# Two instruction orders at the four joins between blocks: products taken whole once both operand halves are there, and VectorE's update chain two tiles deep

## The chip, the cores and the metric

The kernel runs on one core of a Trainium2 chip. The metric is the device time of one execution, in microseconds; below it is given as the median of three runs. Five engines work side by side, each through its own list of instructions: TensorE (PE, the matmuls; PEld is its loading of weights), VectorE (DVE), ScalarE (ACT), GpSimd (POOL) and SyncE (SP, which here only starts transfers). They meet by semaphores: an instruction can wait until a counter has reached a value, and raise one when it is done.

## The reference

The computation is three transformer layers on 512 tokens of width 1024, in float32: layer A (gated delta net and memory attention), layer B (stick-breaking attention and memory attention), and layer C (pooling, differential attention, cross attention). In layers A and B each of the two halves ends in a residual step of this form:

```
y = jnp.concatenate([mix, cross], axis=-1) @ w_out[i]
x = x + rms_norm(y, norm_post_mix[i])
h = rms_norm(x, norm_pre_mlp[i])
y = jnp.square(jax.nn.relu(h @ w_up[i])) @ w_down[i]
x = x + rms_norm(y, norm_post_mlp[i])
```

So `y` is normalised over the tokens' 1024 values, added to `x`, and the new `x`, normalised again, is the operand of the next large product. There are four such joins: after A's output projection (`A.post`, before `A.mlp`), after A's MLP (`A.post2`, before `B.qk`), after B's output projection (`B.post`, before `B.mlp`) and after B's MLP (`B.post2`, before `C.u`). The change concerns these four alone.

## The kernel before

Activations are held turned: 1024 features are 8 tiles (index k, `KD` = 8) of 128 partitions by 512 tokens. `XT` is x, `Y` the output of the last product. Weights come in units of 1024x256 numbers; unit u uses buffers `STG`, `WH`, `WL` number u mod 2, and gives two output tiles (j = 0, 1), each in its own PSUM bank of 128x512.

To keep float32 accuracy with the faster matmul type, each operand is split in a high and a low part: `WH` and `WL` for weights, `HH` and `HL` for activations. A product of one tile k is three matmuls: `HH` with `WH`, `HL` with `WH`, and `HH` with `WL`. A unit is 2 x 8 x 3 = 48 matmuls of 512 columns.

A join runs like this. TensorE sums squares of y over features (`sum_tokens`: eight short matmuls on `SQA`, eight on `SQ`), ScalarE takes the root, VectorE the reciprocal `RSC`, and TensorE spreads it over all partitions into PSUM bank 4 (`spread_tokens`). Then for each k: VectorE scales y (`scaled`, a scalar_tensor_tensor that reads `Y` and bank 4 and writes PSUM bank 5 or 6; line 2008 in the profile, `PS<-Y,PAR,PS`), adds it to x (line 2011, `XT<-XT,PS`); ScalarE makes `HH` of the new tile (line 1330, `HH<-XT,PAR`) and its square for the next norm; VectorE makes `HL` (`operand_lo`, line 2008, `HL<-XT,PAR,HH`). GpSimd meanwhile makes the low weights of unit u+1 (line 421, `WL<-STG,WH`) and then adds up the squares (lines 411 and 415, `SQA`).

Since the sum over features of x is not known until all of x is, the next product is made of x without its norm, and the norm's factor is multiplied in as the result leaves PSUM. TensorE takes units u and u+1 together there (`product_pair`, for the units named in `PAIRED`): as tile k of the operand arrives it does tile k of both outputs of unit u, and one tile-step of unit u+1, so 9 matmuls for each k. After k = 7 come the other eight tile-steps of unit u+1 (n = 8 to 15), and between them the sum (`sum_tokens`) and the spreading (`spread_tokens`) of the next norm. ScalarE copies the spread factor to `RS`, and VectorE then empties the banks of unit u (in an MLP, line 2008, `RR<-PS,RS`). Unit u+2 (`product`) writes to the banks of unit u, and waits until its first one is empty.

The order on each engine is written out by hand in the program; there is no scheduler. In `product_pair` each k is in two parts: `of_hi` waits for `HH` of tile k and does the six matmuls that need it alone, `of_lo` waits for `HL` and does the other three.

Of the kernel before, what the change touches and what calls it, by code (L numbers as in the profile page):

```python
# [27 lines left out]
ALU = mybir.AluOpType  # L28
# [3 lines left out]
P = 128  # L32
S = 512
D = 1024
KD = D // P
# [78 lines left out]
def program(nc, ws, xt_in, memt_in, memt2_in, par_in, con_in, rope_in, rcnt_in, out):  # L114
    ctx = ExitStack()
    with ctx:
        def sb(name, shape, dt=F32, scope=ctx, align=32):
            return scope.enter_context(nc.sbuf_tensor(name, shape, dt, align_bytes=align))

        sems = {}  # L120
# [22 lines left out]
        HL = sb("HL", [P, KD, S], F32R, align=2048)  # L143
        HH = sb("HH", [P, KD, S], F32R)
        XT = sb("XT", [P, KD, S])
        STG = [sb(f"STG{i}", [P, KD, UC]) for i in range(2)]
        WH = [sb(f"WH{i}", [P, KD, UC], F32R) for i in range(2)]
        WL = [sb(f"WL{i}", [P, KD, UC], F32R) for i in range(2)]
        Y = sb("Y", [P, KD, S])
# [10 lines left out]
        PS = ctx.enter_context(nc.psum_tensor("PS", [P, 8, 512], F32))  # L160
# [5 lines left out]
        def par(name, i=0, n=1):  # L166
            return PAR[:, PCOL[name] + i:PCOL[name] + i + n]
# [149 lines left out]
        def emptied(kind, u, j, i=None, step=0):  # L317

            return lin(EMPTIED[kind][u] + j + 1, 2 * step, i)
# [14 lines left out]
        def bcast_done(n):  # L334
            return NORMS.index(n) + 1
# [4 lines left out]
        def split_done(q, k):  # L340
            return 8 * SPLITS.index(q) + k + 1
# [139 lines left out]
        def _(pe):  # L481
            I_ = con("ident")

            def mm(o, l, r, start, stop, **kw):
                return pe.matmul(o, l, r, start=start, stop=stop, **kw)  # L485

            def sum_tokens(name, nt=NB):

                m = SQ_BASE[name] + KD - 1
                pe.wait_ge(sems["sqa"], 6 * sums_done(name))  # L490
                before = [x for x in NORMS if SUMS.index(x) < SUMS.index(name)]
                copied = sum(1 for x in before if x not in POSTS)
                if copied:
                    pe.wait_ge(sems["rs"], copied)
                if before and before[-1] in POSTS:
                    pe.wait_ge(sems["y_scaled"], 8 * POSTS.index(before[-1]) + KD)
                for b in range(nt):
                    mm(PS[:, 4, b:b + 1], blk(SQA[:, :], b), con("ones")[:, 0:1], b == 0, False, skip_group_check=True)
                pe.wait_ge(sems["sq"], m + 1)
                for b in range(nt):  # L500
                    last = mm(PS[:, 4, b:b + 1], blk(SQ[:, m % 4, :], b), con("ones")[:, 0:1], False, True,
                              skip_group_check=True)
                last.then_inc(sems["ss"], 1)

            def spread_tokens(name, nt=NB):

                pe.wait_ge(sems["rsc"], sums_done(name))
                for b in range(nt):
                    last = mm(PS[:, 4, b * P:(b + 1) * P], RSC[:, b:b + 1].to_broadcast([P, P]), I_, True, True)
                last.then_inc(sems["bc"], 1)  # L510

            def wait_bank(u, j, i=None, step=0):

                if u >= 2:
                    kind = KIND[u - 2]
                    pe.wait_ge(sems[f"emptied_{kind}"], emptied(kind, u - 2, j, i, step))
# [42 lines left out]
            def projection(name, split=None, norm=None, after=None, halfway=None, order=range(KD), behind=None, x=(HH, HL)):  # L559


                def fn(u, i, step):
                    r = u - U0[name]
                    first = r == 0 and i is None
                    if first and name in PAIRED:
                        return product_pair(u, split)
                    if r == 1 and name in PAIRED:
                        return
                    product(u, i, step, x[0], x[1],
                            split=(lambda k: split_done(split, k)) if first and split else None,  # L570
                            between=(lambda: spread_tokens(norm)) if norm and r == 1 and i is None else None,
                            tiles=1 if name == "A.bg" else 2, halfway=halfway if first else None, order=order,
                            behind=behind if first else None)
                    if norm and first:
                        sum_tokens(norm)
                    if after and r:
                        after(r - 1)
                run_phase(pe, name, fn)
                if after:
                    after(NU[name] - 1)  # L580

            def product_pair(u, q):

                pe.wait_ge(sems["lo"], u + 1)
                for v in (u, u + 1):
                    wait_bank(v, 0)
                    wait_bank(v, 1)

                def of_hi(v, j, k):
                    bank = PS[:, 2 * (v % 2) + j, :]  # L590
                    wh, wl = WH[v % 2][:, k, j * P:(j + 1) * P], WL[v % 2][:, k, j * P:(j + 1) * P]
                    mm(bank, wh, HH[:, k, :], k == 0, False)
                    mm(bank, wl, HH[:, k, :], False, False)

                def of_lo(v, j, k):
                    bank = PS[:, 2 * (v % 2) + j, :]
                    last = mm(bank, WH[v % 2][:, k, j * P:(j + 1) * P], HL[:, k, :], False, k == KD - 1)
                    if k == KD - 1:
                        last.then_inc(sems["tile"], 1)

                for k in range(KD):
                    pe.wait_ge(sems["hh"], split_done(q, k))
                    of_hi(u, 0, k)
                    of_hi(u, 1, k)
                    if k == 0:
                        pe.wait_ge(sems["lo"], u + 2)
                    of_hi(u + 1, k % 2, k // 2)
                    pe.wait_ge(sems["hl"], split_done(q, k))
                    of_lo(u, 0, k)
                    of_lo(u, 1, k)  # L610
                    of_lo(u + 1, k % 2, k // 2)
                for n in range(KD, 2 * KD):
                    of_hi(u + 1, n % 2, n // 2)
                    of_lo(u + 1, n % 2, n // 2)
                    if n == KD:
                        sum_tokens(q)
                    if n == KD + 4:
                        spread_tokens(q)

            def memory_rows(u, xh, xl, split=None):  # L620
# [1385 lines left out]
        def _(dve):  # L2006
            def stt(o, a, s_, b, op0, op1):
                return dve.scalar_tensor_tensor(out=o, in0=a, scalar=s_, in1=b, op0=op0, op1=op1)  # L2008

            def tt(o, a, b, op):  # L2010
                return dve.tensor_tensor(o, a, b, op)  # L2011
# [7 lines left out]
            def operand_lo(q, src, gain, hh=HH, hl=HL, n=S, k0=0, k1=KD):  # L2019
                for k in range(k0, k1):  # L2020
                    dve.wait_ge(sems["hh"], split_done(q, k))
                    stt(hl[:, k, 0:n], src[:, k, 0:n], par(gain, k), hh[:, k, 0:n].bitcast(F32), ALU.mult, ALU.subtract)\
                        .then_inc(sems["hl"], 1)

            def invert(name, nt=NB):
                dve.wait_ge(sems["sqrt"], sums_done(name))
                dve.reciprocal(RSC[:, 0:nt], RT[:, 0:nt]).then_inc(sems["rsc"], 1)
# [87 lines left out]
            def post_and_operand(post, gain, q, gain_in):  # L2115

                invert(post)
                dve.wait_ge(sems["bc"], bcast_done(post))
                if post in ("A.post", "B.post"):
                    dve.wait_ge(sems["emptied_act"], emptied("act", U0[post[0] + ".out"] + 3, 1))  # L2120
                n = 8 * POSTS.index(post)
                def scaled(k):
                    if k >= 2:
                        dve.wait_ge(sems["x_new"], n + k - 1)
                    stt(PS[:, 5 + k % 2, :], Y[:, k, :], par(gain, k), PS[:, 4, :], ALU.mult, ALU.mult)\
                        .then_inc(sems["y_scaled"], 1)

                scaled(0)
                for k in range(KD):
                    dve.wait_ge(sems["y_scaled"], n + k + 1)  # L2130
                    tt(XT[:, k, :], XT[:, k, :], PS[:, 5 + k % 2, :], ALU.add).then_inc(sems["x_new"], 1)
                    if k + 1 < KD:
                        scaled(k + 1)
                    operand_lo(q, XT, gain_in, k0=k, k1=k + 1)

            def half_top(a, i):
                e, n = i % 2, 8 * a + i
# [354 lines left out]
            for r in range(NU["A.gate"]):  # L2492
                u = U0["A.gate"] + r
# [200 lines left out]
            for r in range(NU["C.out"]):  # L2694
                u = U0["C.out"] + r
# [134 lines left out]
```

## Time and profile before

| | us |
|---|---|
| median of three runs | 2205.88 |
| lowest and highest | 2205.38, 2208.51 |
| profiled execution, its own time | 2205.38 |
| profiled execution, span of the trace | 2203.6 |

| engine | busy, share of the span |
|---|---|
| TensorE, matmuls | 96% |
| TensorE, weight loads | 80% |
| VectorE | 49% |
| ScalarE | 34% |
| GpSimd | 8% |

The profile records one execution. The span is 1.8 us shorter than that execution's own time. TensorE is busy for nearly the whole of it, so what matters is where it is not, and where it is busy at a lower clock: the profile gives the granted clock for any stretch, as a share of full speed (0.50 is the 1.2 GHz level, 1.00 the 2.4 GHz one). The four joins lie at about 417 to 450, 777 to 811, 1054 to 1087 and 1415 to 1447 us of the span.

### The profile page before, as it was taken

The numbers are of one execution on the slowest core, as the hardware profiler recorded it, in microseconds if no ns is written. First come the engines' busy times: TensorE is split into PE (matmuls) and PEld (weight loads), VectorE is DVE, ScalarE is ACT, GpSimd is POOL, SyncE is SP. The second block draws the span as 40 slices with busy tenths as digits, with TensorE's granted clock in tenths as the row PEclk, the third lists the DMA queues.
The fourth block names the chain that finished last, engine by engine and source line by source line (L and its number), as shares of the span: only waits on it lengthen the run. The fifth ranks groups of instructions, "written<-read, shape, count | busy, mean of one in ns | idle before, by whom it ended". The sixth has DMA issues, their size and how long they took to land.

```text
span 2203.6 us, 28778 instructions
## 1 busy us (share of the span) xinstructions
PE 2125.9 (96%) x11819; PEld 1753.5 (80%) x11819; DVE 1084.5 (49%) x1381; ACT 751.0 (34%) x1033; POOL 177.1 (8%) x141
## 2 busy tenths in 40 slices
PE   7999999999999999999999999999899999999998
PEld 6886888788888878767788888787688868888886
DVE  4664555454454453353645445455765335454453
ACT  5444432432122232574422222323462243222222
POOL 2000220300000120001300000401001000000001
PEclk9999999999999999999999999999999999999999
DMA  6231000222222222101222222232132202322221
GB/s 239 77 114 39 22 21 1 77 96 96 95 95 95 97 75 96 39 1 58 76 97 96 95 98 94 104 125 86 58 134 77 81 35 78 113 96 95 95 95 58
DMA packets 27025, 182.81 MB, mean 83 GB/s; under 512 B 2992, under 2 KB 3120, under 8 KB 5424
## 3 DMA queue, kind: packets, MB, share of 16 engines
q1 hardware_dynamic: 25200, 174.07, 22.2%
q10 hardware_dynamic: 1296, 4.71, 0.5%
q0 software_dynamic: 432, 2.62, 0.3%
q8 instruction: 74, 1.21, 0.2%
q14 instruction: 23, 0.19, 0.0%
HBM read 179.30 MB, written 2.10 MB: 82 GB/s over the span
## 4 chain that ended last, share of the span: by engine, by line
PE 89%; DVE 6%; ACT 3%; issue 1%; DMA 0%; POOL 0%; ACTq 0%; DVEq 0%; POOLq 0%; SPq 0%
PE PS L485 88%; ACT Y L1330 1%; DVE Y L2008 1%; ACT WH L1330 1%; DVE WL L2011 1%; DVE Y L2011 1%; DVE SQ L2011 0%; DMA STG<-weights 0%; PE PS L696 0%; DVE DMX L2620 0%; DVE HL L2011 0%; POOL SQA L415 0%; ACT ABUF L1330 0%; ACT SQ L1330 0%; DVE QKV L2011 0%
## 5 line engine op out<-in xcount | busy, mean ns | idle before, releaser
L485 PE MATMUL PS<-HH,WH 128*128 128x512 f32 (+1 forms) x1608 | 635.2, 395 | 17.4 <-ACT HH L1330 10.1
L485 PE MATMUL PS<-HH,WL 128*128 128x512 f32 (+1 forms) x1608 | 625.0, 389 | 0.0
L485 PE MATMUL PS<-HL,WH 128*128 128x512 f32 (+1 forms) x1608 | 613.1, 388 | 0.0
L2011 DVE TENSOR_TENSOR WL<-STG,WH 128x2048 fp32r<-128x2048 f32 (+1 forms) x163 | 367.1, 2252 | 287.0 <-ACT WH L1330 287.0
L1330 ACT ACTIVATE WH<-STG 128x2048 fp32r<-128x2048 f32 (+2 forms) x171 | 314.8, 1841 | 525.9 <-PE PS L485 523.8
L485 PEld LDWEIGHTS PS<-HH,WH 128*128 128x128 f32 x1608 | 305.8, 190 | 90.3 <-issue 22.7
L485 PEld LDWEIGHTS PS<-HH,WL 128*128 128x128 f32 x1608 | 305.9, 190 | 61.3
L485 PEld LDWEIGHTS PS<-HL,WH 128*128 128x128 f32 x1608 | 304.9, 190 | 62.2 <-issue 2.2
L485 PE MATMUL PS<-UPH,WH 128*128 128x512 f32 x832 | 324.2, 390 | 1.4 <-DVE UPL L2008 1.4
L485 PE MATMUL PS<-UPH,WL 128*128 128x512 f32 x832 | 323.7, 389 | 0.0
L485 PE MATMUL PS<-UPL,WH 128*128 128x512 f32 x832 | 323.7, 389 | 0.0
L485 PEld LDWEIGHTS PS<-UPH,WH 128*128 128x128 f32 x832 | 156.2, 188 | 34.1 <-DVE UPL L2008 1.8
L485 PEld LDWEIGHTS PS<-UPH,WL 128*128 128x128 f32 x832 | 156.2, 188 | 32.5
L485 PEld LDWEIGHTS PS<-UPL,WH 128*128 128x128 f32 x832 | 156.2, 188 | 32.3
L411 POOL TENSOR_TENSOR SQA<-SQ 128x512 f32<-128x512 f32 (+1 forms) x14 | 24.9, 1778 | 1594.2 <-ACT SQ L1330 1594.2
L2008 DVE SCALAR_TENSOR_TENSOR RR<-PS,RS 128x512 f32<-128x512 f32 x96 | 66.3, 690 | 146.3 <-PE PS L485 138.4
L2011 DVE TENSOR_TENSOR Y<-Y,PS 128x512 f32<-128x512 f32 x64 | 43.9, 687 | 180.2 <-PE PS L485 180.2
L1330 ACT ACTIVATE UPH<-RR 128x512 fp32r<-128x512 f32 x64 | 40.5, 632 | 226.7 <-DVE RR L2008 226.7
L2011 DVE TENSOR_TENSOR XT<-XT,PS 128x512 f32<-128x512 f32 x80 | 54.6, 683 | 120.2 <-PE PS L485 120.1
L415 POOL TENSOR_TENSOR SQA<-SQA,SQ 128x512 f32<-128x512 f32 (+1 forms) x70 | 97.5, 1393 | 145.2 <-ACT SQ L1330 141.7
L1330 ACT ACTIVATE Y<-PS 128x512 f32<-128x512 f32 (+5 forms) x96 | 61.6, 646 | 86.8 <-PE PS L485 72.1
L2011 DVE TENSOR_TENSOR RQ<-RR 128x512 f32<-128x512 f32 x96 | 66.4, 692 | 3.3
(286 smaller groups left out, 2015.0 us busy)
## 6 DMA issues: line engine op xcount, KB each, us to landing
STG<-weights SPq DMA_DIRECT2D x163, 1024.0 KB, 4.8
XT<-x_t ACTq DMA_DIRECT2D x2, 1024.0 KB, 12.6
out_t<-Y SPq DMA_DIRECT2D x8, 256.0 KB, 2.0
STG<-weights SPq DMA_DIRECT2D x4, 256.0 KB, 5.5
MX<-mem_t ACTq DMA_DIRECT2D x4, 256.0 KB, 7.5
CON<-consts ACTq DMA_DIRECT2D x1, 1024.0 KB, 18.2
Y<-recip_counts POOLq DMA_DIRECT2D x1, 1024.0 KB, 5.0
KVM<-mem_t POOLq DMA_DIRECT2D x1, 1024.0 KB, 8.4
```

The source lines that it names most:

```text
L411: pool.tensor_tensor(SQA[:, 0:n], SQ[:, base % 4, 0:n], SQ[:, (base + 1) % 4, 0:n], ALU.add).then_inc(sems["sqa"], 1)
L415: pool.tensor_tensor(SQA[:, 0:n], SQA[:, 0:n], SQ[:, (base + k) % 4, 0:n], ALU.add).then_inc(sems["sqa"], 1)
L485: return pe.matmul(o, l, r, start=start, stop=stop, **kw)
L1330: return act.activation(o, i, f, **kw)
L2008: return dve.scalar_tensor_tensor(out=o, in0=a, scalar=s_, in1=b, op0=op0, op1=op1)
L2011: return dve.tensor_tensor(o, a, b, op)
```

## The change

Two functions are written in another order. No instruction of arithmetic is added or taken away.

In `product_pair` the two parts become one, `step`: three matmuls for one tile-step in the order `HH` with `WH`, `HL` with `WH`, `HH` with `WL`. Each k waits once, for `HL` of tile k. The sum of the next norm stands after n = 9 (was after 8), its spreading after n = 14 (was after 12).

In `post_and_operand` VectorE's loop runs `scaled` one tile ahead of the addition, and the addition two tiles ahead of `operand_lo`. Before, the addition of tile 0 stood right behind `scaled(0)`, and `operand_lo(k)` right behind `scaled(k + 1)`.

```diff
-                def of_hi(v, j, k):
+                def step(v, j, k):
                     mm(bank, wh, HH[:, k, :], k == 0, False)
-                    mm(bank, wl, HH[:, k, :], False, False)
-
-                def of_lo(v, j, k):
-                    bank = PS[:, 2 * (v % 2) + j, :]
-                    last = mm(bank, WH[v % 2][:, k, j * P:(j + 1) * P], HL[:, k, :], False, k == KD - 1)
+                    mm(bank, wh, HL[:, k, :], False, False)
+                    last = mm(bank, wl, HH[:, k, :], False, k == KD - 1)
...
                 for k in range(KD):
-                    pe.wait_ge(sems["hh"], split_done(q, k))
-                    of_hi(u, 0, k)
-                    of_hi(u, 1, k)
+                    pe.wait_ge(sems["hl"], split_done(q, k))
+                    step(u, 0, k)
+                    step(u, 1, k)
                     if k == 0:
                         pe.wait_ge(sems["lo"], u + 2)
-                    of_hi(u + 1, k % 2, k // 2)
-                    pe.wait_ge(sems["hl"], split_done(q, k))
-                    of_lo(u, 0, k)
-                    of_lo(u, 1, k)
-                    of_lo(u + 1, k % 2, k // 2)
+                    step(u + 1, k % 2, k // 2)
                 for n in range(KD, 2 * KD):
-                    of_hi(u + 1, n % 2, n // 2)
-                    of_lo(u + 1, n % 2, n // 2)
-                    if n == KD:
+                    step(u + 1, n % 2, n // 2)
+                    if n == KD + 1:
                         sum_tokens(q)
-                    if n == KD + 4:
+                    if n == 2 * KD - 2:
                         spread_tokens(q)
...
-                scaled(0)
-                for k in range(KD):
-                    dve.wait_ge(sems["y_scaled"], n + k + 1)
-                    tt(XT[:, k, :], XT[:, k, :], PS[:, 5 + k % 2, :], ALU.add).then_inc(sems["x_new"], 1)
-                    if k + 1 < KD:
-                        scaled(k + 1)
-                    operand_lo(q, XT, gain_in, k0=k, k1=k + 1)
+                for k in range(KD + 2):
+                    if k < KD:
+                        if k >= 2:
+                            dve.wait_ge(sems["x_new"], n + k - 1)
+                        stt(PS[:, 5 + k % 2, :], Y[:, k, :], par(gain, k), PS[:, 4, :], ALU.mult, ALU.mult)\
+                            .then_inc(sems["y_scaled"], 1)
+                    if 1 <= k <= KD:
+                        dve.wait_ge(sems["y_scaled"], n + k)
+                        tt(XT[:, k - 1, :], XT[:, k - 1, :], PS[:, 5 + (k - 1) % 2, :], ALU.add).then_inc(sems["x_new"], 1)
+                    if k >= 2:
+                        operand_lo(q, XT, gain_in, k0=k - 2, k1=k - 1)
```

VectorE at the start of a join (`A.post`), before. `PS<-Y` is `scaled`, `XT<-XT,PS` the addition, `HL` is `operand_lo`; the names in brackets are the semaphores waited for:

```order
L2008 SCALAR_TENSOR_TENSOR PS<-Y,PAR,PS 128x512 [waits emptied_act,bc]
L2011 TENSOR_TENSOR XT<-XT,PS 128x512 [waits y_scaled]
L2008 SCALAR_TENSOR_TENSOR PS<-Y,PAR,PS 128x512
L2008 SCALAR_TENSOR_TENSOR HL<-XT,PAR,HH 128x512 [waits hh]
L2011 TENSOR_TENSOR XT<-XT,PS 128x512 [waits y_scaled]
```

The same place with the change:

```order
L2000 SCALAR_TENSOR_TENSOR PS<-Y,PAR,PS 128x512 [waits emptied_act,bc]
L2000 SCALAR_TENSOR_TENSOR PS<-Y,PAR,PS 128x512
L2003 TENSOR_TENSOR XT<-XT,PS 128x512 [waits y_scaled]
L2000 SCALAR_TENSOR_TENSOR PS<-Y,PAR,PS 128x512 [waits x_new]
L2003 TENSOR_TENSOR XT<-XT,PS 128x512 [waits y_scaled]
L2000 SCALAR_TENSOR_TENSOR HL<-XT,PAR,HH 128x512 [waits hh]
```

`HL` of tile 0 stood behind one addition and two `scaled`; now it stands behind two additions and three `scaled`, and the third of these waits for the first addition.

TensorE at the start of the pair that follows, before (`WH0`, `WL0` are the buffers of unit u, `WH1`, `WL1` those of unit u+1):

```order
L485 MATMUL PS<-CON,RSC 128x128 x3
L485 MATMUL PS<-HH,WH0 128x512 [waits emptied_act,hh,lo]
L485 MATMUL PS<-HH,WL0 128x512
L485 MATMUL PS<-HH,WH0 128x512
L485 MATMUL PS<-HH,WL0 128x512
L485 MATMUL PS<-HH,WH1 128x512 [waits lo]
L485 MATMUL PS<-HH,WL1 128x512
L485 MATMUL PS<-HL,WH0 128x512 [waits hl]
```

And with the change:

```order
L485 MATMUL PS<-CON,RSC 128x128 x3
L485 MATMUL PS<-HH,WH0 128x512 [waits emptied_act,hl,lo]
L485 MATMUL PS<-HL,WH0 128x512
L485 MATMUL PS<-HH,WL0 128x512
L485 MATMUL PS<-HH,WH0 128x512
L485 MATMUL PS<-HL,WH0 128x512
L485 MATMUL PS<-HH,WL0 128x512
L485 MATMUL PS<-HH,WH1 128x512 [waits lo]
```

Six matmuls stood ahead of the wait for `hl`; now all nine stand behind it.

TensorE from the spreading of the next norm to the first matmul of unit u+2, before (`CON,RSC` is the spreading, `WH0` now unit u+2):

```order
L485 MATMUL PS<-CON,RSC 128x128 [waits rsc]
L485 MATMUL PS<-CON,RSC 128x128 x3
L485 MATMUL PS<-HH,WH1 128x512
L485 MATMUL PS<-HH,WL1 128x512
L485 MATMUL PS<-HL,WH1 128x512
L485 MATMUL PS<-HH,WH1 128x512
L485 MATMUL PS<-HH,WL1 128x512
L485 MATMUL PS<-HL,WH1 128x512
L485 MATMUL PS<-HH,WH1 128x512
L485 MATMUL PS<-HH,WL1 128x512
L485 MATMUL PS<-HL,WH1 128x512
L485 MATMUL PS<-HH,WH0 128x512 [waits emptied_dve,lo]
```

With the change:

```order
L485 MATMUL PS<-CON,RSC 128x128 [waits rsc]
L485 MATMUL PS<-CON,RSC 128x128 x3
L485 MATMUL PS<-HH,WH1 128x512
L485 MATMUL PS<-HL,WH1 128x512
L485 MATMUL PS<-HH,WL1 128x512
L485 MATMUL PS<-HH,WH0 128x512 [waits emptied_dve,lo]
```

Between the spreading and the wait for the emptied bank stood nine matmuls; now there are three.

## Rows read from the trace of the kernel before

**Rows 1.** The chain that ended last, by engine, from the page.

```profile
PE 89%; DVE 6%; ACT 3%; issue 1%; DMA 0%; POOL 0%; ACTq 0%; DVEq 0%; POOLq 0%; SPq 0%
```

**Rows 2.** TensorE's waits: what for, us in total, times, longest.

```profile
PE PS L485 <- ACT HH L1330: 10.1, 4, 2.6
```

**Rows 3.** Timeline of TensorE, starts of the four pairs: start, us, instruction, [idle before].

```profile
422.81 0.76 PE L485 MATMUL PS<-HH,WH 128*128 128x512 f32 x1 [2.55 <-ACT HH L1330]
...
783.79 0.77 PE L485 MATMUL PS<-HH,WH 128*128 128x512 f32 x1 [2.47 <-ACT HH L1330]
...
1059.72 0.77 PE L485 MATMUL PS<-HH,WH 128*128 128x512 f32 x1 [2.56 <-ACT HH L1330]
...
1420.95 0.77 PE L485 MATMUL PS<-HH,WH 128*128 128x512 f32 x1 [2.48 <-ACT HH L1330]
```

**Rows 4.** Timeline of VectorE, start of the first join.

```profile
420.37 0.76 DVE L2008 SCALAR_TENSOR_TENSOR PS<-Y,PAR,PS 128x512 f32<-128x512 f32 x1 [1.32 <-ACT Y L1330]
421.16 0.69 DVE L2011 TENSOR_TENSOR XT<-XT,PS 128x512 f32<-128x512 f32 x1
421.77 0.75 DVE L2008 SCALAR_TENSOR_TENSOR PS<-Y,PAR,PS 128x512 f32<-128x512 f32 x1
422.70 2.25 DVE L2008 SCALAR_TENSOR_TENSOR HL<-XT,PAR,HH 128x512 fp32r<-128x512 f32 x1 [0.18 <-ACT HH L1330]
424.87 0.67 DVE L2011 TENSOR_TENSOR XT<-XT,PS 128x512 f32<-128x512 f32 x1
...
426.33 0.75 DVE L2008 SCALAR_TENSOR_TENSOR HL<-XT,PAR,HH 128x512 fp32r<-128x512 f32 x1
427.00 0.68 DVE L2011 TENSOR_TENSOR XT<-XT,PS 128x512 f32<-128x512 f32 x1
```

**Rows 5.** Timeline of GpSimd, low weights of unit u+1 at the four joins.

```profile
419.86 4.54 POOL L421 TENSOR_TENSOR WL<-STG,WH 128x2048 fp32r<-128x2048 f32 x1 [6.50 <-ACT WH L1330]
...
779.99 4.52 POOL L421 TENSOR_TENSOR WL<-STG,WH 128x2048 fp32r<-128x2048 f32 x1 [6.34 <-ACT WH L1330]
...
1056.76 4.52 POOL L421 TENSOR_TENSOR WL<-STG,WH 128x2048 fp32r<-128x2048 f32 x1 [6.50 <-ACT WH L1330]
...
1417.49 4.52 POOL L421 TENSOR_TENSOR WL<-STG,WH 128x2048 fp32r<-128x2048 f32 x1 [6.34 <-ACT WH L1330]
```

**Rows 6.** Timeline of TensorE, two neighbours early in the first pair.

```profile
423.37 0.63 PE L485 MATMUL PS<-HH,WL 128*128 128x512 f32 x1
423.80 0.63 PE L485 MATMUL PS<-HH,WH 128*128 128x512 f32 x1
```

**Rows 7.** One stretch early in the first pair: us, TensorE busy, granted clock, DMA.

```profile
423.00:424.00 1.00, 1.00 (x3) 0.50 0.00 0
```

**Rows 8.** Timeline of TensorE, first matmuls of the next norm's sum, four pairs.

```profile
442.08 0.95 PE L485 MATMUL PS<-CON,SQA 128*128 128x1 f32 x8
...
803.40 0.95 PE L485 MATMUL PS<-CON,SQA 128*128 128x1 f32 x8
...
1079.58 0.95 PE L485 MATMUL PS<-CON,SQA 128*128 128x1 f32 x8
...
1439.66 0.95 PE L485 MATMUL PS<-CON,SQA 128*128 128x1 f32 x8
```

**Rows 9.** Timeline of TensorE, the spreading and the first matmuls of unit u+2.

```profile
446.65 1.05 PE L485 MATMUL PS<-CON,RSC 128*128 128x128 f32 x8
...
449.62 0.39 PE L485 MATMUL PS<-HH,WH 128*128 128x512 f32 x1
449.84 0.39 PE L485 MATMUL PS<-HL,WH 128*128 128x512 f32 x1
```

**Rows 10.** Timeline of ScalarE and VectorE behind that spreading.

```profile
447.74 0.60 ACT L1330 ACTIVATE RS<-PS 128x512 f32<-128x512 f32 x1 [3.51 <-PE PS L485]
...
448.37 0.69 DVE L2008 SCALAR_TENSOR_TENSOR RR<-PS,RS 128x512 f32<-128x512 f32 x1 [2.54 <-ACT RS L1330]
```

**Rows 11.** Timeline of GpSimd, its first addition of squares.

```profile
426.89 1.34 POOL L411 TENSOR_TENSOR SQA<-SQ 128x512 f32<-128x512 f32 x1 [2.50 <-ACT SQ L1330]
```

More of the change, by code:

```diff
@@ L2121, in post_and_operand @@
                 n = 8 * POSTS.index(post)
-                def scaled(k):
-                    if k >= 2:
-                        dve.wait_ge(sems["x_new"], n + k - 1)
-                    stt(PS[:, 5 + k % 2, :], Y[:, k, :], par(gain, k), PS[:, 4, :], ALU.mult, ALU.mult)\
-                        .then_inc(sems["y_scaled"], 1)
-                scaled(0)
-                for k in range(KD):
-                    dve.wait_ge(sems["y_scaled"], n + k + 1)
-                    tt(XT[:, k, :], XT[:, k, :], PS[:, 5 + k % 2, :], ALU.add).then_inc(sems["x_new"], 1)
-                    if k + 1 < KD:
-                        scaled(k + 1)
-                    operand_lo(q, XT, gain_in, k0=k, k1=k + 1)
+                for k in range(KD + 2):
[7 more added lines that the diff above has]
+                        tt(XT[:, k - 1, :], XT[:, k - 1, :], PS[:, 5 + (k - 1) % 2, :], ALU.add).then_inc(sems["x_new"], 1)
+                    if k >= 2:
+                        operand_lo(q, XT, gain_in, k0=k - 2, k1=k - 1)
             def half_top(a, i):
```

## The prediction

> **What bounds the kernel now.** I read the shares of the chain that ended last first. TensorE has 89% of it [rows 1], so the change can act only where TensorE idles, waits or runs slowly. Next came TensorE's waits. The largest group is exactly the place that the change rewrites: four waits for `HH`, 10.1 us together, one at the start of each pair [rows 2, 3]. Then I read the timelines of that place. After its start the pair shows no further idle time: from the first matmul to the first one of the next norm's sum TensorE has 75 matmuls of 512 columns (9 for each of eight k, 3 for n = 8), and takes 19.27, 19.61, 19.86 and 18.71 us for them in the four places [rows 3, 8]. At the full rate of 0.227 us each (0.22 to 0.23 between neighbours [rows 9]) 75 would take 17.03. The rest, 2.24, 2.58, 2.83 and 1.68 us, in all 9.33, is the low clock at the start: the granted clock is 0.50 there, the 1.2 GHz level, after a wait of 2.5 us and short matmuls before it [rows 3, 7], and neighbours stand 0.43 us apart [rows 6].
>
> VectorE delivers one tile of `HL` each 2.13 us (from one addition to the next, 424.87 to 427.00 [rows 4]); TensorE at full rate uses one in 9 x 0.227 = 2.04. So the supply is a little slower than the use. But TensorE has lost 1.7 to 2.8 us at the low clock, against 7 x 0.09 = 0.6 us that the supply falls behind over seven tiles. TensorE's own work sets the pair's end, and that end moves with its start.
>
> **Term 1, the later start.** The first matmul waited for `HH` of tile 0; now it waits for `HL` of tile 0, which VectorE also reaches later. Call T0 the start of `scaled(0)`, 420.37 in the first place [rows 4]. The first matmul came at T0 + 2.44 [rows 3, 4]. I take the same 2.44 in the other places, so T0 is 781.35, 1057.28 and 1418.51 there. Spacing on VectorE: from an `HL` to the addition behind it 0.67, from an addition to the next instruction 0.61 [rows 4]; `scaled` is of the same form as `HL`, so I take 0.67 behind it. In the new order:
> - `scaled(0)` at T0, `scaled(1)` at T0 + 0.67, the first addition at T0 + 1.34, ended at T0 + 2.03 (0.69 long).
> - `scaled(2)` waits for that end (about 0.03 more, as between the first two rows): T0 + 2.06. The second addition at T0 + 2.73.
> - `HL` of tile 0 at T0 + 3.33. It needs `HH`, which is there 1.54 after the start of the first addition (421.16 to 422.70 [rows 4]), so at T0 + 2.88: no wait.
> - Unhindered it takes 0.75, to T0 + 4.08. TensorE starts about 0.11 after what it waits for (422.70 to 422.81 [rows 3, 4]): T0 + 4.19, or 1.75 later than before.
>
> In the row this instruction took 2.25 and not 0.75: it ended at 424.95, that is 0.55 after the end of GpSimd's `WL` at 424.40 [rows 4, 5]. The new start, 423.70 in the first place and 1060.61 in the third, still lies inside GpSimd's instruction (to 424.40 and 1061.28), so the end stays at 424.95 and becomes 1061.83. TensorE then starts at 425.06 and 1061.94, which is 2.25 and 2.22 later. In the second place GpSimd ends at 784.51, before 784.68: 1.75. In the fourth it ends at 1422.01, just behind 1421.84, and 0.55 after that is 1422.56, as good as the unhindered end of 1422.59: 1.75. Sum 2.25 + 1.75 + 2.22 + 1.75 = 8.0 us. Bounds: 7.0 if nothing holds `HL` (4 x 1.75), 9.0 if all four are held as long as the first (4 x 2.25).
>
> The Trainium skill (SBUF — State Buffer, "SBUF: two separate sides") says that a VectorE instruction with two SBUF inputs and a GpSimd instruction that reads SBUF lock each other out for the whole instruction, whichever began first. The 2.25 us row agrees. By that rule the new order has a second collision, weighed as a rival below.
>
> **The clock after the start.** The wait ahead of the pair grows from 2.5 to some 4.5 us, so the clock is low at the start as before. What the low clock costs I take as before, 9.33 in all, so nothing in the sum. Bounds from the same rows: the least place four times is 4 x 1.68 = 6.7 (2.6 less), the dearest 4 x 2.83 = 11.3 (2.0 more).
>
> **What the shorter VectorE cycle brings.** `HL(k)` no longer stands waiting for `HH(k)`: 0.61 + 0.67 + 0.67 = 1.95 a tile in place of 2.13. Over seven tiles that is 1.3 us, but it comes on an engine that TensorE does not wait for once it has started. I count nothing. Having one wait per k in place of two is also nothing: neither kind shows idle time behind the first.
>
> **Term 2, the spreading moved to the end.** Unit u+2 writes the bank that VectorE empties, and VectorE needs `RS`, which ScalarE copies after the spreading. From the start of the spreading S (446.65) the copy starts at S + 1.09, the emptying at S + 1.72 and ends at S + 2.41 [rows 9, 10]. With 0.1 for TensorE's reaction, the bank is free at S + 2.51. Before, TensorE wanted it at 449.62, S + 2.97 [rows 9]: hidden, by 0.46. Two tile-steps (6 x 0.23 = 1.38) now stand ahead of the spreading and not behind it, so it wants it at S + 1.59. A stall of 0.92 appears, four times: 3.7 us. Queued behind the waiting matmul is all of TensorE's further work. Bounds: 4 x 0.8 = 3.2 with no reaction time, and 4 x 1.2 = 4.8 if some more comes late. The sum one tile-step later costs nothing: the reciprocal hangs on VectorE's `WL` of unit u+2, and the spreading moved by more than the sum did.
>
> **Sum.** 8.0 + 3.7 = 11.7 us. The profiled execution took 2205.38, with a span of 2203.6 and 1.8 around it that stays. That gives 2217.1. The median of the runs shown is 0.5 higher; I say 2217.3.
>
> **The rivals.**
> - *The clock rises at the same moment as before, however late TensorE starts.* Then of a later start only the part that would have run at full rate is lost: a matmul done at the low rate would have taken 0.43 and is done later in 0.227, so 0.227 / 0.43 = 0.53 of the delay remains, 8.0 x 0.53 = 4.2. With term 2: 7.9, 2213.3. For it: the low stretch differs between places (1.68 to 2.83) though the wait ahead of them is the same. Against: it would have to hold in all four. Chance 12%.
> - *The stall in front of unit u+2 does not come*, because the bank is released sooner than the rows say: only term 1, 2213.4. Against: the copy and the emptying are one chain behind the spreading, with 2.41 us in a row each. Chance 6%.
> - *VectorE meets GpSimd's additions of squares.* An addition of squares starts 2.02 after x of its tile does and takes 1.34 (424.87 to 426.89 [rows 4, 11]), so until + 3.36. Before, `HL(k)` began at + 1.46, ahead of it. Now it comes 1.95 + 0.61 = 2.56 after, inside it. Held as in the first row, it ends at + 3.91 and not at + 3.31; two cycles then take 4.5, so 2.25 a tile. `HL(7)` comes 15.8 after `HL(0)`, and TensorE's step k = 7 stands 12 matmuls ahead of the sum, so 16.0 to 17.1 after its start: still in time. It decides from about 2.3 a tile on. Were every cycle held by a further 0.6, so 2.8, `HL(7)` would come at 19.6, on average 3 us late: 4 x 3 more, 2229. Chance 4%. This is the lock of the Trainium skill's page again; by its rule each `HL` but the first and last is held once, which is the harmless case.
> - *The other side, not slower: the end of each pair is set by the last `HL`.* Then the shorter cycle ends it 7 x (2.13 - 1.95) = 1.3 us sooner where `HL(0)` ends when it did (first and third place), and at best so in all four: - 5.2, with term 2 added - 1.5, 2203.9. For it: 2.13 is more than 2.04. Against: it decides only where the low clock costs less than 0.6 us, and the least is 1.68; and even wholly at full rate, 17.03 after its new start, the pair in the first place would be at 442.09, where it was at 442.08. Chance 3%.
>
> **How the numbers follow.** The forecast has 75%, the rivals 12, 6, 4 and 3. Range: the lower bounds give 7.0 - 2.6 + 3.2 = 7.6, 2213.0; the upper ones 9.0 + 2.0 + 4.8 = 15.8, 2221.2. That takes in the first two rivals. What a measurement can tell from no change is about 0.2%, 4.4 us: slower by more than that means over 2210.3. All cases but the last lie above it; a clock that comes back sooner together with a smaller stall could end inside it. Slower 92%, within 5%, faster 3%.
>
> **What would show it.** TensorE's wait at the start of each pair now ends on VectorE's `HL`, near 4.8 us in the first and third place and 4.2 in the others. `HL(0)` starts 1.0 later against T0, with 2.25 shrunk to about 1.25 in the first place. Four new waits of 0.9 stand in front of unit u+2, on VectorE's first emptying. VectorE's cycle is 1.95, or 2.25 if GpSimd's additions hold it. The distance from a pair's first matmul to its sum is the old one plus one tile-step of 0.68. The prediction is wrong if that distance shrinks by more than a microsecond a place, if TensorE waits inside the eight steps, or if the bank is free when it asks.

## The result, and the profile after

The changed kernel took 2229.09 us (median of 4 runs, 2225.30 to 2230.28) against 2206.73 (4 runs): ratio 1.0096, 95% interval 1.0081 to 1.0111. Slower, as forecast, but by 22 us where 11.7 were forecast, and outside the range. The sign and both terms of the sum were right; the step that failed, the one that took everything outside the joins as fixed, is told below. The profiled execution is quicker than every timed run: 2221.33, with a span of 2219.5 against 2203.6, so 15.9 more.

TensorE's waits after, the rows that answer to [rows 2] (what for, us, times, longest):

```profile
PE PS L485 <- DVE HL L2000: 19.1, 5, 4.8
...
PE PS L485 <- DVE RR L2000: 1.6, 2, 0.8
...
PE PS L485 <- DVE QKB L2000: 0.8, 1, 0.8
PE PS L485 <- DVE UT L2003: 0.8, 1, 0.8
```

The four waits for `HH` are gone. In their place are four longer waits for `HL`, 18.2 us together (the fifth of that row, 0.9, stood in the kernel before too), and four new ones of 0.8 for VectorE's first emptying of a bank. The timeline of TensorE shows the four starts, to set against [rows 3]:

```profile
427.18 0.77 PE L485 MATMUL PS<-HH,WH 128*128 128x512 f32 x1 [4.81 <-DVE HL L2000]
...
791.60 0.77 PE L485 MATMUL PS<-HH,WH 128*128 128x512 f32 x1 [4.23 <-DVE HL L2000]
...
1069.83 0.76 PE L485 MATMUL PS<-HH,WH 128*128 128x512 f32 x1 [4.40 <-DVE HL L2000]
...
1433.44 0.77 PE L485 MATMUL PS<-HH,WH 128*128 128x512 f32 x1 [4.81 <-DVE HL L2000]
```

VectorE in the first join, against [rows 4]:

```profile
422.48 1.41 DVE L2000 SCALAR_TENSOR_TENSOR PS<-Y,PAR,PS 128x512 f32<-128x512 f32 x2 [1.32 <-ACT Y L1322]
423.80 0.68 DVE L2003 TENSOR_TENSOR XT<-XT,PS 128x512 f32<-128x512 f32 x1
424.51 0.76 DVE L2000 SCALAR_TENSOR_TENSOR PS<-Y,PAR,PS 128x512 f32<-128x512 f32 x1
425.18 0.68 DVE L2003 TENSOR_TENSOR XT<-XT,PS 128x512 f32<-128x512 f32 x1
425.78 1.26 DVE L2000 SCALAR_TENSOR_TENSOR HL<-XT,PAR,HH 128x512 fp32r<-128x512 f32 x1
```

T0 is 422.48. `HL` starts at T0 + 3.30 (forecast 3.33) and TensorE at T0 + 4.70 (4.69). The 1.26 us of `HL` are GpSimd's hold again, now shorter, because `HL` comes later. The first matmuls of the next norm's sum, against [rows 8]:

```profile
447.70 0.95 PE L485 MATMUL PS<-CON,SQA 128*128 128x1 f32 x8
...
810.90 0.95 PE L485 MATMUL PS<-CON,SQA 128*128 128x1 f32 x8
...
1089.91 0.95 PE L485 MATMUL PS<-CON,SQA 128*128 128x1 f32 x8
...
1452.67 0.94 PE L485 MATMUL PS<-CON,SQA 128*128 128x1 f32 x8
```

These come 20.52, 19.30, 20.08 and 19.23 us after their pair's start. The sum now stands one tile-step (0.68) later, so like for like 19.84, 18.62, 19.40 and 18.55, against 19.27, 19.61, 19.86 and 18.71: 1.0 us less in all. And the end of the first pair, against [rows 9]:

```profile
452.94 1.05 PE L485 MATMUL PS<-CON,RSC 128*128 128x128 f32 x8
...
455.50 0.47 PE L485 MATMUL PS<-HH,WH 128*128 128x512 f32 x1 [0.80 <-DVE RR L2000]
```

From the spreading to unit u+2 it takes 2.56, where 2.51 was forecast, and 0.80 of it is idle.

Cut at the same landmarks (first matmul of the norm's sum ahead of a join; first matmul of unit u+2 behind it, which before is the spreading + 2.97), the traces of the kernel before (this one and e8_before_copy) and of the changed kernel (this one, e5_full_again, e9_full_third) read:

| stretch | before, two traces | changed, three traces | difference of means |
|---|---|---|---|
| start to first join | 416.64, 420.29 | 418.74, 415.55, 424.46 | varies |
| join 1 | 32.98, 32.97 | 36.76, 36.65, 36.65 | + 3.7 |
| join 2 | 34.91, 34.89 | 36.63, 36.61, 36.63 | + 1.7 |
| join 3 | 33.58, 33.54 | 36.31, 36.23, 36.19 | + 2.7 |
| join 4 | 33.67, 33.67 | 36.22, 36.19, 36.22 | + 2.5 |
| between the joins | 895.4, 895.4 | 895.8, 895.9, 895.8 | + 0.4 |
| behind join 4 | 756.4, 756.3 | 759.0, 759.0, 759.0 | + 2.7 |

All but the first line repeats to 0.1 us or so. It adds up to 13.7 us for the change: 10.7 in the joins, 0.4 between them, 2.7 behind them. The first line is 13.5 us wide over all the traces of this study, and no line of the change acts there.

### The profile page after: what moved, and what is told of

It reads as the page before. It is cut to its first block, busy times and chain, and to the rows that moved or that the text cites. A ratio compares the mean times of both kernels' runs of the same rounds, so it can differ in the third digit from the quotient of the medians.

```text
span 2219.5 us, 28778 instructions
## 1 busy us (share of the span) xinstructions
PE 2127.8 (96%) x11819; PEld 1755.6 (79%) x11819; DVE 1087.5 (49%) x1381; ACT 750.5 (34%) x1033; POOL 176.7 (8%) x141
## 3 DMA queue, kind: packets, MB, share of 16 engines
q1 hardware_dynamic: 25200, 174.07, 22.4%
## 4 chain that ended last, share of the span: by engine, by line
PE 88%; DVE 6%; ACT 3%; issue 1%; DMA 1%; POOL 0%; ACTq 0%; DVEq 0%; POOLq 0%; SPq 0%
PE PS L485 87%; ACT Y L1322 2%; DVE Y L2000 1%; ACT WH L1322 1%; DVE Y L2003 1%; DVE WL L2003 1%; DMA MX<-mem_t 0%; DVE SQ L2003 0%; DVE PS L2000 0%; DMA STG<-weights 0%; PE PS L688 0%; DVE HL L2000 0%; DVE DMX L2610 0%; DVE HL L2003 0%; POOL SQA L415 0%
## 5 line engine op out<-in xcount | busy, mean ns | idle before, releaser
L485 PE MATMUL PS<-HL,WH 128*128 128x512 f32 (+1 forms) x1608 | 624.7, 388 | 0.0
L2003 DVE TENSOR_TENSOR XT<-XT,PS 128x512 f32<-128x512 f32 x80 | 54.5, 681 | 121.7 <-PE PS L485 121.7
```

## The experiments

For the first four experiments three theories stood against each other. L: the joins cost what the prediction says, and the low clock behind the longer wait costs the rest. V: VectorE's new order is what costs. N: the excess over the joins is chance of the runs. From e5_full_again on two took their place. P: the joins cost 10.8, and the rest of the first measurement is low clock in the stage ahead of the first join, where nothing was changed. E: an excess of 9 us over the joins belongs to the change.

**e1_pe_only.** TensorE's part of the change, VectorE in the old order:

```diff
...
                 for k in range(KD):
-                    pe.wait_ge(sems["hh"], split_done(q, k))
+                    pe.wait_ge(sems["hl"], split_done(q, k))
...
-                    if n == KD + 4:
+                    if n == 2 * KD - 2:
```

> TensorE's part alone (whole steps behind one wait for HL, later sum and spreading), VectorE in the old order. Theory L (later start, late spreading, and a dearer low clock behind the longer wait): the first matmul comes 2.2, 1.4, 2.2, 1.7 us later than before (7.5 in all), unit u+2 waits 0.8 four times (3.2), and the timed runs lie above that sum by most of what the full change lies above it: 2218 to 2228. Theory V (VectorE's new order is what costs): under 2212. Theory N (the excess over the joins is chance of the runs and not of the change): 2217.5.

Measured 2220.63 against 2210.01, ratio 1.0074 (1.0051 to 1.0097). The starts were 2.25, 1.40, 2.24 and 2.32 later against T0, 8.2 in all; the joins took 146.5 us, 11.4 more than before. The 11.4 are these 8.2 and the late spreading, 3.8, less 0.6 by which T0 comes sooner in the fourth join, so TensorE's part alone makes the whole cost in the joins, and theory V is out. What VectorE's old order could give back (it reaches `HL` of tile 0 sooner) was lost in the first, third and fourth join to GpSimd's hold: in the first, `HL` of tile 0 is asked for at T0 + 2.32 and takes 2.22 us.

```profile
423.33 2.22 DVE L2000 SCALAR_TENSOR_TENSOR HL<-XT,PAR,HH 128x512 fp32r<-128x512 f32 x1 [0.18 <-ACT HH L1322]
```

**e2_dve_only.** VectorE's part, TensorE in the old order:

```diff
...
-                scaled(0)
-                for k in range(KD):
...
+                for k in range(KD + 2):
...
```

> VectorE's part alone, TensorE in the old order. Theory L: HH of tile 0 is ready 0.55 us later, so four starts move by 0.55: 2.2 us, 2209, and no dearer clock since the wait is only 3 us. Theory V: 2216 or more. If the shorter VectorE cycle brings something here, it is under 2206.

Measured 2216.64 against 2210.01, ratio 1.0025 (1.0006 to 1.0045); joins 138.6, 3.5 more. The starts were 0.52 later in each place (2.1 in all, 2.2 expected). The expected 2209 was missed, and 2216 was theory V's number. But the kernel before ran 3.3 us slower here than the expectations assume: as a difference the time, some 5.5 us with an interval from 1.3 to 9.9, lies between theory L's 2.3 and theory V's 9.3 and takes in both. The trace speaks for the small cost. TensorE waited 3.00 to 3.08 us for `HH` in place of 2.5:

```profile
432.61 0.77 PE L485 MATMUL PS<-HH,WH 128*128 128x512 f32 x1 [3.07 <-ACT HH L1330]
```

**e3_old_places.** The changed kernel, sum and spreading where they stood before:

```diff
-                    if n == KD + 1:
+                    if n == KD:
...
-                    if n == 2 * KD - 2:
+                    if n == KD + 4:
```

> The changed kernel, but with the sum and the spreading of the next norm where they stood before (after n = 8 and n = 12). Theory L: the four waits of 0.80 us in front of unit u+2 go, 3.2 us less than the full change: some 2224 to 2226 against 2227 to 2229. If the late spreading were behind the excess too, it is under 2220.

Measured 2222.21, ratio 1.0055 (1.0034 to 1.0076). No wait in front of unit u+2 was left; joins 143.3, 2.4 less than the changed kernel (3.2 expected). The times alone don't settle it: 12.2 us over the kernel before, with an interval from 7.5 to 16.8, takes in the 13.3 below which the late spreading would be behind the excess, and lies under theory L's 17.3 to 19.3. The trace does: putting sum and spreading back saves 2.4 us in the joins, not the 10.7 by which the first measurement stood over the forecast.

**e4_places_only.** The kernel before with only the places moved:

```diff
-                    if n == KD:
+                    if n == KD + 1:
...
-                    if n == KD + 4:
+                    if n == 2 * KD - 2:
```

> The kernel before, with only the places of sum and spreading moved (after n = 9 and n = 14). Theory L: four waits of 0.8 us and nothing else, 2210. If the late spreading is behind the excess: 2214 or more.

Measured 2215.18, ratio 1.0015 (0.9998 to 1.0032), which can't be told from no change; joins 137.8, 2.7 more. The moved places cost 3.8 by themselves, but T0 came 0.9 us sooner in the second join and 0.6 sooner in the fourth. The wait is there in each place, alone and of the forecast size:

```profile
457.73 1.05 PE L485 MATMUL PS<-CON,RSC 128*128 128x128 f32 x8
460.29 0.47 PE L485 MATMUL PS<-HH,WH 128*128 128x512 f32 x1 [0.81 <-DVE RR L2008]
```

In this batch the kernel before ran 22 times, from 2203.93 to 2216.75: 13 us wide, where its first four runs lay within 3.1. The expectations of this batch are reckoned from 2206.7, its median in the first measurement; the differences are what can be compared.

**e5_full_again.** The changed kernel once more, without an edit.

> The changed kernel itself, once more, beside more runs of the kernel before. Theory P (the joins cost 10.8 us as the first trace shows, the rest of the first measurement is the low clock in the stage before the first join, which no line of the change touches and which falls differently from run to run): the ratio comes out near 1.005 to 1.007, the times of both kernels scatter by 10 us or more, and in this trace too the four joins from the first sum to unit u+2 take 10 to 12 us more than before, while the arrival at the first join follows the low-clock time ahead of it at about 0.46 us per us. Theory E (the excess of 9 us over the joins belongs to the change): the ratio is 1.009 or more again.

Measured 2223.42 against 2210.29, ratio 1.0066 (1.0040 to 1.0092); joins 145.7. Theory P's value; theory E's 1.009 lies inside the interval too, so this alone settles nothing. The arrival at the first join was 415.55, 3.2 us earlier than in the first trace of the same kernel.

**e6_keep_before** and **e7_keep_full.** Extra matmuls in TensorE's waits of the joins, in the kernel before and in the changed one (`keep(22)` there behind the spreading):

```diff
             def finish_post(name):
                 sum_tokens(name)
...
+                def keep(n):
+                    for _ in range(n):
+                        mm(PS[:, 7, 0:UC], WH[u % 2][:, 0, 0:P], WH[u % 2][:, 1, :], True, True)
+
+                keep(3)
                 spread_tokens(name)
+                keep(12)
```

> The kernel before, with extra matmuls (128 weights, 256 columns, results unused, bank 7) in TensorE's waits at each join: 3 ahead of the wait for the reciprocal, 12 behind the spreading. They take some 0.11 us each at the full rate and 0.21 at the low one. If they hold the clock up, the 75 matmuls of the pair take 17.0 us in place of 18.7 to 19.9, the starts move by at most 0.5 each, and the kernel gains 5 to 9 us. If the clock falls all the same, it loses 0 to 2 us.

> The changed kernel with the same extra matmuls, 22 behind the spreading since the wait is longer. If they hold the clock up, the later start (8.0) and the wait in front of unit u+2 (3.2) stand alone: 11 us more than e6_keep_before and about 1 to 4 more than the kernel before. If the low clock behind the longer wait were what makes the change dear (theory L's excess), the gain here is larger than in e6_keep_before by several us.

e6_keep_before: 2214.45, ratio 1.0009 (0.9993 to 1.0025). The expectation (5 to 9 us gained) failed in an instructive way. The clock did stay high in the first three joins, and in the first (first row: us, busy time of PE, PEld, DVE, ACT, POOL, granted clock, DMA share, GB/s) the pair was not shorter:

```profile
429.00:449.00 20.00, 18.82 (x80) 13.93 (x80) 15.74 (x21) 10.45 (x17) 13.44 (x8) 1.00 0.16 53
```

```profile
429.28 0.47 PE L485 MATMUL PS<-HH,WH 128*128 128x512 f32 x1 [1.11 <-ACT HH L1343]
...
430.96 0.51 PE L485 MATMUL PS<-HH,WH 128*128 128x512 f32 x1 [0.51 <-POOL WL L421]
...
432.87 0.51 PE L485 MATMUL PS<-HH,WH 128*128 128x512 f32 x1 [0.39 <-ACT HH L1343]
...
448.57 0.95 PE L485 MATMUL PS<-CON,SQA 128*128 128x1 f32 x8
```

448.57 - 429.28 is 19.29, at the full rate all along; before it was 19.27 with a start at the low one. TensorE now waits for GpSimd's low weights and for `HH` of the next tile instead: VectorE's cycle of 2.14 us a tile paces the pair. In the second and third pair, also at the full rate, the distance to the sum is 18.42 and 18.74, 1.2 and 1.1 less than before, with the same 2.14 a tile; there GpSimd holds `HL` of tile 0 for less. In the fourth the clock fell all the same (granted 0.50 from 1428 to 1430 us), and its distance is 19.62, 0.9 more. All four joins together took 133.7, 1.4 less than before.

e7_keep_full: 2219.61, ratio 1.0036 (1.0017 to 1.0055); joins 141.7, 4 less than the changed kernel and 8.0 more than e6_keep_before (11 expected); against the kernel before it takes some 8 us more, where 1 to 4 were expected. Its pairs reach the sum 18.52, 18.55, 19.42 and 18.50 after their start, 0.68 of it the moved sum. In the first, second and fourth the clock stayed high: about 17.85 like for like, 0.8 over the 17.03 of matmuls alone. In the third it fell (granted 0.50 from 1076 to 1078 us). So the extra matmuls gave 4.0 us here and 1.4 in the kernel before: the low clock behind the longer wait is dearer by 2.6 us over four joins, not by 9. Theory L falls.

**e8_before_copy** and **e9_full_third.** Both kernels without an edit, side by side.

> The kernel before against itself. It shows how far two sets of runs of one kernel lie apart, and gives a second trace of its joins. Theory P: the ratio is 1.000 with an error of about 0.002, the four joins take 134 to 137 us from first sum to unit u+2 (135.1 in the first trace), and the rest of the span follows the low-clock time outside the joins. Theory E needs a ratio within 0.001 of 1, so that 9 us of excess in the first measurement can't be chance.

> The changed kernel a third time, beside the copy of the kernel before. Theory P: joins 145 to 147 us, ratio 1.0045 to 1.007, and against runs of the kernel before at the same mean clock 11 us more. Theory E: 1.009 or more.

e8_before_copy: ratio 1.0004 (0.9989 to 1.0019), joins 135.1 as in the first trace. That ratio is what both theories asked for. e9_full_third: 2224.10 against 2209.93, ratio 1.0059 (1.0039 to 1.0079), joins 145.7: theory E's 1.009 lies outside. Ahead of the first join the trace of e9_full_third stands against that of e5_full_again, the same kernel (one row each of the stretch 0 to 415 us, columns as above):

```profile
0.00:415.00 415.00, 389.75 (x3430) 327.28 (x3431) 219.58 (x380) 171.56 (x324) 48.34 (x65) 0.95 0.20 73
```

```profile
0.00:415.00 415.00, 388.95 (x3469) 327.70 (x3470) 222.14 (x381) 174.02 (x326) 50.37 (x66) 0.98 0.21 76
```

The granted clock is 0.95 and 0.98, and fewer instructions are done by 415 us in the first. Adding up the low-clock time ahead of the first join from stretches of 2 us, over all the traces:

| low clock ahead of join 1, us | 17 | 20 | 20 | 24 | 27 | 34 | 37 | 37 | 41 | 41 | 41 | 48 |
|---|---|---|---|---|---|---|---|---|---|---|---|---|
| arrival, us | 415.55 | 416.64 | 417.27 | 418.74 | 420.29 | 423.11 | 424.46 | 424.69 | 425.92 | 426.38 | 426.38 | 429.09 |
| kernel | e5 | before | e1 | after | e8 | e6 | e9 | e10 | e2 | e4 | e7 | e3 |

(429.09 - 415.55) / 30.6 = 0.44 us of arrival for each us of low clock, close to the 0.47 that a matmul of 512 columns loses there (0.43 against 0.227). The kernels' order in this table has nothing to do with their edits.

The timed runs have no trace, but each has a mean clock. At the same mean clock:

| mean clock | kernel before: runs, mean us | changed kernel: runs, mean us | difference |
|---|---|---|---|
| 0.977 | 4, 2218.2 | 6, 2228.4 | 10.2 |
| 0.978 | 2, 2216.5 | 4, 2225.6 | 9.1 |
| 0.980 | 11, 2212.5 | 5, 2221.4 | 8.9 |

These differences are under the 11 that theory P expected and the 13.7 of the traces, and the traces say why. Behind the arrival at the first join they have 54.6 and 54.5 us of low clock in the kernel before, and 64.8, 64.7 and 64.9 in the changed one. A run of the changed kernel at the same mean clock so had 10.2 us less of it ahead, and by the table above arrived 10.2 x 0.44 = 4.5 us sooner. 13.7 - 4.5 is 9.2.

Over all runs of the study the kernel before has a mean of 2210.5 (68 runs, those beside the experiments), the changed one 2225.2 (19 runs): 14.7 us, 0.66%. Seven of the 19 are from the first measurement. The 12 of e5_full_again and e9_full_third alone have a mean of 2224.1, against 2210.6 for the 58 of the kernel before in those two batches: 13.5 us, as the traces say.

**e10_best.** A try at a version better than both: e6_keep_before, five more extra matmuls ahead of the last squares behind an MLP, and on VectorE

```diff
...
+                scaled(0)
+                added_to_x(0)
+                scaled(1)
+                added_to_x(1)
+                for k in range(KD):
                     operand_lo(q, XT, gain_in, k0=k, k1=k + 1)
...
```

> The kernel before with the extra matmuls of e6_keep_before (and five more ahead of the last squares in the joins behind an MLP), and on VectorE the second addition moved ahead of the first HL, while GpSimd holds that one off anyway. e6_keep_before showed that a pair at full clock is paced by VectorE: 19.3 us to the sum, as at the low clock. The moved addition should bring HL of tiles 1 to 7 forward by up to 0.6 us in the joins where HL of tile 0 is held (all four at high clock), so the joins take 130 to 132 us against 133.7, and the kernel gains 2 to 5 us on before, 0.1 to 0.2%.

Measured 2214.42 against 2209.93, ratio 1.0013 (0.9996 to 1.0029); joins 133.3, 1.8 less than before and 0.4 less than e6_keep_before; 130 to 132 were expected. No gain that can be measured, and the time is not better. From join 4 to the end it took 758.8 us where the kernel before takes 756.4: what the joins gave was lost there, as in e6_keep_before (760.4). No version of this study beats the kernel before.

## Why the prediction was right or wrong, point by point

**Term 1, the later start: right.** Against T0 the starts came 2.26, 1.75, 1.92 and 2.33 later, 8.3 for 8.0. GpSimd's hold behaved as read: full in the first place, none in the second. In the third T0 itself came 0.3 late, behind a spreading at the low clock (T0 is 4.07 after the join's first sum, before 3.74), while GpSimd's instruction did not, so less of `HL` was held (1.92 for 2.22). In the fourth T0 came 0.6 sooner, so more was held (2.33 for 1.75).

**Term 2, the wait in front of unit u+2: right.** From the sum to unit u+2 it takes 7.80 with the sum 0.68 later, against 7.54: 0.94 each, 3.8 for 3.7. Alone, in e4_places_only, each wait is 0.8 too.

**"TensorE's own work sets the pair's end": right for the kernel before, but with far less room than argued, without harm to the sum.** In the first three pairs of the kernel before every step of nine matmuls behind the low clock takes 2.04 to 2.06 us, the full rate without a wait; in the fourth the last two take 2.07 and 2.15, so there the supply had already caught up. The argument set 1.7 to 2.8 us of low clock against 0.6 that the supply falls behind, and left out what GpSimd's hold takes from the supply at the start, up to 1.5 us (2.25 for an `HL` of 0.75). e6_keep_before ran the first pair at full clock and took 19.29, with 2.14 a step. Supply and the low clock set nearly the same end there, and taking one away leaves the other. Of the 9.33 us that I put down to the low clock, two places gave 1.2 and 1.1 and the first nothing; the joins gained 1.4 in all. The fourth rival's condition ("only where the low clock costs less than 0.6 us") was wrong for the same reason: in the fourth place the low clock cost 1.68 and the supply showed. The rival's time did not come.

**The clock after the start, and the shorter VectorE cycle, "nothing": nearly.** Pairs took 1.0 us less in all: 0.57 more, 0.99 less, 0.46 less and 0.16 less. The 0.99 is just inside the microsecond a place that the prediction named as a sign of being wrong. VectorE's cycle was neither 1.95 nor an even 2.25 but 2.01 and 2.44 in turn (starts of additions 427.62, 429.62, 432.06), every second `HL` held by GpSimd's addition for 0.5 us, the others for under 0.1. The mean of 2.22 is that of the rival on GpSimd's squares, and harmless as computed there.

**"A span of 2203.6 and 1.8 around it that stays": this is the step that failed.** It took everything outside the joins as fixed, in two ways.
- Behind join 4 the changed kernel takes 2.7 us more in all three traces, where no instruction was changed. Some 1.6 of it arise at the start of the cross-attention's output projection, where the clock falls now and did not before; the other 1.0 in the last norm, where the spreading runs at the low rate. Eight microseconds around that start, before and after, and that spreading, before and after:

```profile
1790.00:1798.00 8.00, 5.29 (x20) 3.38 (x19) 4.44 (x8) 5.36 (x10) 0.00 (x0) 1.00 0.00 0
```

```profile
1804.00:1812.00 8.00, 5.29 (x15) 3.58 (x14) 4.90 (x8) 5.36 (x10) 0.00 (x0) 0.79 0.00 0
```

```profile
2193.94 1.16 PE L485 MATMUL PS<-CON,RSC 128*128 128x128 f32 x8 [0.57 <-DVE RSC L2027]
```

```profile
2208.86 2.08 PE L485 MATMUL PS<-CON,RSC 128*128 128x128 f32 x8 [0.56 <-DVE RSC L2019]
```

  Dearer joins alone do not bring this with them. e1_pe_only, whose joins cost 11.4 more, takes only 0.3 more behind join 4: the clock stays at 1.00 at that projection. e3_old_places, with joins 8.2 dearer, has the fall there (0.82 over the same eight microseconds, 1.5 us), but 1.4 us less low clock shortly before, and ends 0.1 over the kernel before. Why the clock falls where it does in each arrangement is open.

- The stage ahead of the first join takes 415 to 429 us from one execution to the next, by how much of it the clock is low. My baseline of 2205.38 was one execution with little of it, and the range had no term for it. The first comparison set four runs of the kernel before, 2205.4 to 2208.5 (range over the study 2203 to 2219), against timed runs of the changed one with mean clocks of 0.976 to 0.978, the low end of what that kernel showed in 19 runs (0.975 to 0.982). That is where the other 8 of its 22 us lie: the kernel before's median there was 3.9 us under its mean in the last two batches, the changed one's 5.0 over its own, and 22.4 - 8.9 is 13.5. That the first comparison caught both kernels at opposite ends of their scatter is luck, and shown; that it was this stage in just those runs is argued from the traces of others, since they have no trace of their own.

So the change costs 10.7 us in the joins (11.7 forecast), 13.7 with what came between and behind them, and 14.7 over all runs. The 10.7 came so near with some luck: starts and waits cost 0.4 more than forecast, the pairs gave 1.0 back, and T0 came 0.3 sooner over the four joins. The first measurement's interval, 1.0081 to 1.0111, holds neither; the study gives 0.6 to 0.7%. Theory P was nearest, but it had no term for the 2.7 us behind the joins; theory E's ratio of 1.009 was not seen again in two measurements. Of the rivals, none gave the time. The third one's mechanism, `HL` held by the additions of squares, came in its harmless form.

## What to carry to other kernels

Where an operand comes in two halves, let the matmuls that need only the first run while the second is made; waiting once for both costs the whole distance between them, at each join. Before calling an engine the bound of a stretch, compute the end by the supply as well: two limits a fraction of a microsecond apart hide each other, and removing one gives little or nothing. And take the spread of the unchanged stages from several traces before setting a range, cutting every trace at the same landmarks: 10.7 us in 2210 stand out to 0.1 us that way, where whole runs scatter by 13.

## What the runs showed of the hardware that was not expected

From trace to trace of the same kernel the joins repeat to 0.1 us or so, low clock included. The pairs took 19.27, 19.61, 19.86, 18.71 and in e8_before_copy 19.26, 19.59, 19.83, 18.70, though the first join was reached 3.65 us later; in the three traces of the changed kernel no pair differs by more than 0.2. So in these traces the place where the clock falls in the joins belonged to the arrangement of the program and was no matter of luck. The change in the joins went with a fall of the clock at the cross-attention's output projection, some 345 us behind the last join, in all three traces of the changed kernel and in neither of the kernel before.

Wherever VectorE's `HL`, which reads two operands in SBUF, was held by GpSimd, it ended 0.55 us (0.55 or 0.56 by the records) after GpSimd's instruction did: 4 held ones in the joins of the kernel before and 25 in the changed kernel's first trace (2.25 and 1.26 us for the same 0.75 us instruction). `scaled`, which reads `Y` in SBUF and bank 4 in PSUM, ran its usual 0.76 us meanwhile (424.51 in the first join). The Trainium skill (SBUF — State Buffer, "SBUF: two separate sides") calls this an exclusive lock for the whole instruction; the rows agree.
